# Sparse attention in pairs: the two heads of a feature block on two halves of TensorE's array

## The chip, the cores and the metric

The kernel runs on one core of a Trainium2 chip. The metric is the device time of one execution in microseconds (us). All data and all arithmetic of the part looked at here are float32.

## What is computed

The reference is two transformer stacks behind each other. The change touches one layer of the first stack, a sparse attention (NSA) over 512 tokens with 16 heads of 64 features, four heads sharing one group of keys and values. Each head attends three times: over 31 compressed blocks (`cmp`), over selected blocks (`slc`) and over a window (`win`). With 512 tokens there are 8 blocks of 64 and the top 16 are selected, so the selection takes all of them, and the window of 512 takes all earlier tokens: both are causal attention with a linear distance bias, each with keys and values of its own.

```
def nsa_attention(q, kc, vc, ks, vs, kw, vw, gate_logit, ...):
    ck = compress_kv(kc...)
    cv = compress_kv(vc...)
    ...
        sc = jnp.einsum('bqgrd,bcgd->bgrqc', qb, ck).astype(f32) * scale
        sc = jnp.where(ok_c, sc - slopes[:, :, None, None] * dist_c, NEG_INF)
        p_cmp = jnp.where(jnp.any(ok_c, axis=-1)[:, None], jax.nn.softmax(sc, axis=-1), 0.0)
        o_cmp = jnp.einsum('bgrqc,bcgd->bqgrd', p_cmp.astype(dt), cv)
        ...
        ss = jnp.einsum('bqgrd,bgqnld->bgrqnl', qb, kg).astype(f32) * scale
        ss = jnp.where(dist_s[:, :, None] >= 0, ss - slopes[...] * dist_s[:, :, None], NEG_INF)
        p_slc = jax.nn.softmax(ss.reshape(...), axis=-1).reshape(ss.shape)
        o_slc = jnp.einsum('bgrqnl,bgqnld->bqgrd', p_slc.astype(dt), vg)
        ...
        p_win = jax.nn.softmax(sw, axis=-1)
        o_win = jnp.einsum('bgrqk,bkgd->bqgrd', p_win.astype(dt), vwb)
        o = gb[..., 0:1] * o_cmp + gb[..., 1:2] * o_slc + gb[..., 2:3] * o_win
```

## The kernel before

Activations lie feature-major in SBUF: a feature block is 128 partitions by 512 tokens, and in this layer a block `pr` (0 to 7) of the queries holds two heads, `e` = 0 in partitions 0 to 63 and `e` = 1 in partitions 64 to 127 (`half(e)`). The list `NSA` (L338) writes out by hand the order of the work. Its entries are 128 jobs `("job", pr, i, e, br)`: query tile `i` (0 to 3, 128 queries) of head `e` against the `128*(i+1)` keys at or before it, for branch `br` (0 `slc`, 1 `win`); and 8 entries `("cmp", pr)`, the compressed branch of both heads and all query tiles of a block at once. Two query tiles alternate, 3 with 0 and then 2 with 1. The four jobs and the compressed part of one (pr, i) form a group `G`, which adds up its output in one PSUM bank.

Each job goes through six steps on three engines. TensorE: `scores` (L1311) writes queries times keys into one of three PSUM banks. VectorE: `highest` (L2716, the work at L2741) adds the distance bias, writes the result to `Sbuf` (four buffers) and keeps the row's extreme. ScalarE: `exps` (L2062) takes the exponential and the row sum. VectorE: `normalise` (L2744, reciprocal L2759, scaling by gate and sum L2761). TensorE: `turn` (L1327) transposes the rows in pieces of 128x128. ScalarE: `turned` (L2071, copy at L2082) brings them from PSUM to `PTbuf` (three buffers). TensorE: `values` (L1339) multiplies with the values at L1353 and adds into the group's bank; the first job of a group also adds the compressed part (L1350). When a group is complete, VectorE copies the bank out (`output`, L2763).

A scores matmul contracts over 64 partitions only, those of its head. A values matmul yields 64 features, but uses 128 columns of weights: `vpad_s` and `vpad_w` hold 192 columns for each key tile and group, the values in columns 64 to 127 and zeros on both sides, and a slice at 64 or at 0 puts the values into the lower or the upper half while zeros are added to the other half.

On TensorE the loop of slot n (L1361) issues scores(n+2), turn(n-2), values(n-3). Into 24 slots a quarter of a query projection is put, two matmuls 512 wide (`query_quarter`, L1299, `Q_PART`; slots 0 to 7 and every fifth up to 83). The waits that set the order: scores(n) waits for highest of job n-3, turn(n) for normalise(n) and for the copy of job n-2, values(n) for its own copy. highest(n) waits for scores(n) and for turn(n-4), whose buffer it takes. ScalarE issues exps(n) and then turned(n-2). VectorE issues highest(n), normalise(n-1), output(n-4), and near the end of the layer sums of weights and of inputs for the layer's output product `c_out` (n = 100, 101, 120, 124).

A float32 matmul is two instructions in the trace, each with a load of weights in front; a transpose is one.

Of the kernel before, what the change touches and what calls it, by code (L numbers as in the profile page):

```python
# [161 lines left out]
def build(nc, x_dram, mem_in, meta_in, w_tiles, w_narrow, w_cmp, consts, pick_halves, params, out, stop=None):  # L162
    ctx = ExitStack()
    with ctx:
# [148 lines left out]
        def half(h):  # L313
            return slice(64 * (h % 2), 64 * (h % 2) + 64)
# [24 lines left out]
        for _pr in range(8):  # L339
            for _a, _b in ((3, 0), (2, 1)):  # L340
                for _br, _e in ((0, 0), (0, 1), (1, 0), (1, 1)):
                    NSA += [("job", _pr, _i, _e, _br) for _i in (_a, _b)]
                if _a == 3 and _pr < 7:
                    NSA.append(("cmp", _pr + 1))
        NSA_JOB = [sum(t[0] == "job" for t in NSA[:n]) for n in range(len(NSA))]
        NSA_GROUPS = [(pr, i) for pr in range(8) for i in (3, 0, 2, 1)]
        CMP_AT = [NSA.index(("cmp", pr)) for pr in range(8)]
# [436 lines left out]
        def _(pe):  # L784
# [433 lines left out]
            def nsa():  # L1218
# [92 lines left out]
                def scores(n):  # L1311
                    if n >= 3:
                        pe.wait_ge(na_max, n - 2)
                    ps = sc_bank[n % 3]
                    if NSA[n][0] == "cmp":
                        pr = NSA[n][1]
                        arrived(pr)
                        for i in range(4):
                            mm = pe.matmul(ps[:, 64 * i:64 * i + 64], Z1[:, pr, P * i:P * i + P],
                                           ck[:, pr // 2].rearrange("p e n -> p (e n)"), start=True, stop=True)  # L1320
                    else:
                        _, pr, i, e, br = NSA[n]
                        mm = pe.matmul(ps[:, 0:P * (i + 1)], Z1[half(e), pr, P * i:P * i + P],  # L1323
                                       Z1[half(e), nsa_keys(pr, e, br), 0:P * (i + 1)], start=True, stop=True)
                    mm.then_inc(na_s, 1)
# [13 lines left out]
                def values(n):  # L1339
                    if NSA[n][0] == "cmp":  # L1340
                        return
                    _, pr, i, e, br = NSA[n]
                    g, G = pr // 2, nsa_group(pr, i)
                    o = PL[:, 2 * (G % 2), 0:P]
                    pe.wait_ge(na_pt, n + 1)
                    if (e, br) == (0, 0):
# [4 lines left out]
                    pad = slice(64, 192) if e == 0 else slice(0, 128)  # L1351
                    for j in range(i + 1):
                        mm = pe.matmul(o, (vpad_s, vpad_w)[br][:, j, g, pad], PTbuf[NSA_JOB[n] % N_BANK][:, P * j:P * j + P],  # L1353
                                       start=False, stop=(e, br) == (1, 1) and j == i)
                    mm.then_inc(na_v, 1)
# [3 lines left out]
                scores(0)  # L1359
                scores(1)  # L1360
                for n in range(len(NSA) + 3):  # L1361
                    if n + 2 < len(NSA):
                        scores(n + 2)
                    if n in Q_PART:
                        query_quarter(*Q_PART[n])
                    if 2 <= n < len(NSA) + 2:
                        turn(n - 2)
                    if n >= 3:
                        values(n - 3)
# [400 lines left out]
        def _(act):  # L1770
# [240 lines left out]
            def nsa(ready):  # L2011
# [59 lines left out]
                def turned(n):  # L2071
# [8 lines left out]
                    if m >= N_BANK:  # L2080
                        act.wait_ge(na_v, m - N_BANK + 1)
                    act.activation(PTbuf[m % N_BANK][:, 0:w], pt_bank[n % 2][:, 0:w], ACT.Copy).then_inc(na_pt, 1)  # L2082
# [282 lines left out]
        def _(dve):  # L2365
# [330 lines left out]
            def nsa():  # L2696
# [66 lines left out]
                def output(n):  # L2763
                    if NSA[n][0] == "cmp" or NSA[n][3:] != (1, 1):
                        return
# [4 lines left out]
                for n in range(len(NSA) + 4):  # L2770
# [6 lines left out]
                    if n >= 4:  # L2777
                        output(n - 4)
# [754 lines left out]
```

## Time and profile before

| | |
|---|---|
| median of 3 runs | 3782.35 us (3779.25 to 3784.62) |
| the profiled execution | 3778.26 us, its span 3776.4 us |
| busy share PE, DVE, ACT | 97%, 52%, 20% of the span |
| granted TensorE clock, mean | 0.978 (1.00 in the attention stage) |
| the attention stage | 1128 to 1420 us of the span, 292 us |
| in it: PE, DVE, ACT busy | 291.8, 174.0, 135.4 us |

A row of the timeline merges neighbouring instructions of a line: its start, the time to the end of the last, engine, line, operation, names, shapes (weights, then moving data) and count. Ends of matmuls are modelled (a matmul's record runs on over the start of the next), so what a block of matmuls costs TensorE is read from the start of one row to the start of the next row of PE. PEld is the load of weights.

### The profile page before, as it was taken

To read this page: it belongs to the slowest core of one execution; us is meant where nothing else is said; L and a number is where in the kernel's file an instruction comes from. 1 tells how busy PE (TensorE), PEld (TensorE's weight loads), DVE (VectorE), ACT (ScalarE), POOL (GpSimd) and SP (SyncE) were. 2 spreads that over 40 slices of the span, in tenths; PEclk is the share of its full clock that TensorE was granted. 3 is DMA by queue.
4 is the path that set the end of the run, shared out by engine and by line. 5 is a ranking of instruction groups with operands and counts; after the bars stand their busy time and mean duration, and the time that the engine had idled before them with its cause. 6 is when DMAs were issued, how large, how long until landed. Compare 5 with 4: busy or idle time off the path is not lost.

```text
span 3776.4 us, 43884 instructions
## 1 busy us (share of the span) xinstructions
PE 3658.8 (97%) x16715; PEld 2855.7 (76%) x16715; DVE 1978.3 (52%) x4623; ACT 757.3 (20%) x1849; POOL 70.5 (2%) x74
## 2 busy tenths in 40 slices
PE   8987999999999999999998999999999999999999
PEld 3374788888655668888886776888887888887766
DVE  4362366545205574675545547643344566557456
ACT  2221021100113451111001135022112111121143
POOL 0000000000000000000000011000000000000010
PEclk9998999999999999999998999999999999999999
DMA  3100312222210003212222110221110122101111
GB/s 125 56 12 25 120 56 79 89 89 90 100 45 12 12 12 112 78 68 90 86 82 78 67 45 23 81 76 67 45 45 34 67 78 85 39 23 68 56 45 45
DMA packets 35014, 236.83 MB, mean 63 GB/s; under 512 B 4716, under 2 KB 4844, under 8 KB 7168
## 3 DMA queue, kind: packets, MB, share of 16 engines
q1 hardware_dynamic: 31616, 224.41, 16.8%
q10 hardware_dynamic: 2704, 5.46, 0.4%
q0 software_dynamic: 496, 4.24, 0.3%
q8 instruction: 134, 2.20, 0.2%
q14 instruction: 64, 0.52, 0.0%
HBM read 232.00 MB, written 2.10 MB: 62 GB/s over the span
## 4 chain that ended last, share of the span: by engine, by line
PE 94%; DVE 4%; ACT 1%; issue 1%; DMA 0%; POOL 0%; ACTq 0%; POOLq 0%; DVEq 0%
PE PL L1193 25%; PE PX L1193 19%; PE PL L901 14%; PE PL L1572 4%; PE PL L1385 3%; PE PX L1323 2%; PE PL L885 2%; PE PL L1353 2%; PE PX L1675 2%; PE PL L1596 1%; PE PL L1306 1%; PE PL L1480 1%; PE PL L1718 1%; PE PX L1455 1%; PE PX L911 1%
## 5 line engine op out<-in xcount | busy, mean ns | idle before, releaser
L901 PE MATMUL PL<-xn,ring 128*128 128x264 f32 (+1 forms) x1600 | 508.8, 475 | 11.0 <-DVE xn L2394 9.8
L901 PEld LDWEIGHTS PL<-xn,ring 128*128 128x128 f32 x1600 | 306.5, 194 | 197.7 <-issue 164.8
L2437 DVE TENSOR_TENSOR Z<-PL,SCR 128x512 f32<-128x512 f32 (+3 forms) x104 | 63.9, 615 | 489.0 <-PE PL L901 377.6
L1193 PE MATMUL PL<-Z,ring 128*128 128x256 f32 (+1 forms) x1248 | 299.2, 391 | 2.1 <-POOL Z L3392 2.1
L1193 PEld LDWEIGHTS PL<-Z,ring 128*128 128x128 f32 x1248 | 242.8, 195 | 42.2 <-POOL Z L3392 2.4
L1193 PE MATMUL PL<-AUX,ring 128*128 128x256 f32 (+1 forms) x1056 | 243.9, 379 | 0.0
L1193 PEld LDWEIGHTS PL<-AUX,ring 128*128 128x128 f32 x1056 | 200.6, 190 | 27.6
L1193 PE MATMUL PL<-xn,ring 128*128 128x264 f32 (+1 forms) x864 | 204.3, 389 | 15.7 <-DVE xn L2394 14.5
L1193 PEld LDWEIGHTS PL<-xn,ring 128*128 128x128 f32 x864 | 165.8, 192 | 46.0 <-issue 12.4
L1849 ACT ACTIVATE SCR<-PL 128x256 f32<-128x256 f32 (+1 forms) x72 | 27.7, 384 | 739.1 <-PE PL L1193 739.1
L1193 PE MATMUL PX<-Z,AUX 128*128 128x264 f32 (+1 forms) x704 | 163.8, 384 | 0.5 <-DVE Z L3168 0.5
L1572 PE MATMUL PL<-xn,ring 128*128 128x264 f32 x640 | 154.1, 395 | 0.0
L1193 PE MATMUL PX<-AUX,ring 128*128 128x256 f32 (+1 forms) x640 | 152.5, 381 | 0.0
L1193 PEld LDWEIGHTS PX<-Z,AUX 128*128 128x128 f32 x704 | 133.7, 190 | 22.0 <-issue 0.8
L2584 DVE TENSOR_TENSOR SCR<-SCR,PL 128x256 f32<-128x256 f32 (+1 forms) x72 | 30.4, 422 | 214.3 <-PE PL L1193 214.3
L1572 PEld LDWEIGHTS PL<-xn,ring 128*128 128x128 f32 x640 | 121.5, 193 | 27.9 <-issue 7.9
L1193 PEld LDWEIGHTS PX<-AUX,ring 128*128 128x128 f32 x640 | 121.6, 190 | 17.8
L1819 ACT ACTIVATE SCR<-resid 128x512 f32<-128x512 f32 (+1 forms) x88 | 53.8, 632 | 384.2 <-DVEq L2626 239.7
L1385 PE MATMUL PL<-xn,ring 128*128 128x264 f32 x512 | 121.0, 393 | 0.0
L1385 PEld LDWEIGHTS PL<-xn,ring 128*128 128x128 f32 x512 | 98.7, 193 | 17.9 <-issue 0.7
L1323 PE MATMUL PX<-Z 64*128 64x512 f32 (+3 forms) x256 | 102.5, 481 | 0.0
L1849 ACT ACTIVATE AUX<-PL 128x264 f32<-128x264 f32 x44 | 17.2, 390 | 412.9 <-PE PL L1193 412.9
(517 smaller groups left out, 6386.1 us busy)
## 6 DMA issues: line engine op xcount, KB each, us to landing
ring<-w_tiles SPq DMA_DIRECT2D x212, 1024.0 KB, 4.8
cst<-consts ACTq DMA_DIRECT2D x1, 2252.5 KB, 15.0
resid<-x ACTq DMA_DIRECT2D x4, 512.0 KB, 8.3
AUX<-mem POOLq DMA_DIRECT2D x2, 1024.0 KB, 5.2
AUX<-w_cmp POOLq DMA_DIRECT2D x1, 2048.0 KB, 10.3
out<-resid SPq DMA_DIRECT2D x4, 512.0 KB, 5.1
par<-params ACTq DMA_DIRECT2D x1, 536.5 KB, 6.2
nar<-w_narrow ACTq DMA_DIRECT2D x1, 368.0 KB, 17.0
```

The source lines that it names most:

```text
L885: mm = pe.matmul(PL[:, 2 * h + c, 0:e - a], ring[t % 2][:, k, P * h:P * h + P], src[:, KB * kc + k, a:e], start=kc == 0 and k == 0, stop=k ...
L901: mm = pe.matmul(PL[:, 2 * h + c, 0:e - a], ring[t % 2][:, k, P * h:P * h + P], src_block(name, k)[:, a:e], start=k == 0, stop=k == KB - 1)
L911: mm = pe.matmul(PX[0:G, at + c, 0:e - a], K("sum_row", 7 - b // N["per"], 7 - b // N["per"] + G), sq_buf[:, bb % 4, a:e], start=b == 0, s ...
L1193: mm = pe.matmul(ps, lhs(k), rhs(k), start=kc == 0 and k == 0, stop=kc == per - 1 and k == 3)
L1323: mm = pe.matmul(ps[:, 0:P * (i + 1)], Z1[half(e), pr, P * i:P * i + P], Z1[half(e), nsa_keys(pr, e, br), 0:P * (i + 1)], start=True, stop ...
L1353: mm = pe.matmul(o, (vpad_s, vpad_w)[br][:, j, g, pad], PTbuf[NSA_JOB[n] % N_BANK][:, P * j:P * j + P], start=False, stop=(e, br) == (1, 1 ...
L1385: mm = pe.matmul(PL[:, 2 * h + c, 0:e - a], ring[t % 2][:, k, P * h:P * h + P], X2[:, k, a:e], start=k == 0, stop=k == KB - 1)
L1572: mm = pe.matmul(PL[:, 2 * c, 0:HALF], ring[t % 2][:, k, P * (u % 2):P * (u % 2) + P], X2[:, k, c * HALF:(c + 1) * HALF], start=k == 0, st ...
L1675: mm = pe.matmul(ps, k, q, start=True, stop=True)
L1819: act.activation(sq, src[b], ACT.Square).then_inc(norm_sq, 1)
L1849: act.activation(quad_work(name)[2 + n % 2], quad_bank(name, "m1"), ACT.Copy).then_inc(qd_c, 1)
L2437: ins = dve.tensor_tensor(d, ps, f, ALU.mult)
```

## The change

Jobs of the two heads of one (pr, i, br) become neighbours in `NSA` and form a unit; an entry `cmp` is a unit alone. TensorE's loop goes by units: scores of unit k+1 (both heads behind each other, in two banks), both turns of unit k-1, values of unit k-2. The values matmul takes the 64 columns that hold values and writes half of the partitions of the output; for each key tile the two heads' matmuls alternate, e = 0 into partitions 0 to 63, e = 1 into 64 to 127. The number of jobs, the turns, and all that VectorE and ScalarE do for a job stay as they are. There are four `PTpair` buffers in place of three `PTbuf`, and `output` is moved two slots back.

```
--- before.py
+++ after.py
@@ -338,12 +338,14 @@
         NSA = [("cmp", 0)]
         for _pr in range(8):
             for _a, _b in ((3, 0), (2, 1)):
-                for _br, _e in ((0, 0), (0, 1), (1, 0), (1, 1)):
-                    NSA += [("job", _pr, _i, _e, _br) for _i in (_a, _b)]
+                for _br in range(2):
+                    NSA += [("job", _pr, _i, _e, _br) for _i in (_a, _b) for _e in range(2)]
                 if _a == 3 and _pr < 7:
                     NSA.append(("cmp", _pr + 1))
         NSA_JOB = [sum(t[0] == "job" for t in NSA[:n]) for n in range(len(NSA))]
         NSA_GROUPS = [(pr, i) for pr in range(8) for i in (3, 0, 2, 1)]
+        NSA_UNITS = [(n,) if t[0] == "cmp" else (n, n + 1) for n, t in enumerate(NSA) if t[0] == "cmp" or t[3] == 0]
+        PTpair = [SCR[:, 512 * (N_S + j):512 * (N_S + j + 1)] for j in range(4)]
         CMP_AT = [NSA.index(("cmp", pr)) for pr in range(8)]
         C_FIRST = 14
         Q_SLOTS = list(range(8)) + [8 + 5 * j for j in range(16)]
@@ -1308,21 +1310,23 @@
                     if part == 3:
                         mm.then_inc(lin_done, 1)
 
-                def scores(n):
-                    if n >= 3:
-                        pe.wait_ge(na_max, n - 2)
+                def scores(unit):
+                    n = unit[0]
                     ps = sc_bank[n % 3]
+                    if unit[-1] >= 3:
+                        pe.wait_ge(na_max, unit[-1] - 2)
                     if NSA[n][0] == "cmp":
                         pr = NSA[n][1]
                         arrived(pr)
                         for i in range(4):
                             mm = pe.matmul(ps[:, 64 * i:64 * i + 64], Z1[:, pr, P * i:P * i + P],
                                            ck[:, pr // 2].rearrange("p e n -> p (e n)"), start=True, stop=True)
-                    else:
+                        mm.then_inc(na_s, 1)
+                        return
+                    for n in unit:
                         _, pr, i, e, br = NSA[n]
-                        mm = pe.matmul(ps[:, 0:P * (i + 1)], Z1[half(e), pr, P * i:P * i + P],
-                                       Z1[half(e), nsa_keys(pr, e, br), 0:P * (i + 1)], start=True, stop=True)
-                    mm.then_inc(na_s, 1)
+                        pe.matmul(sc_bank[n % 3][:, 0:P * (i + 1)], Z1[half(e), pr, P * i:P * i + P],
+                                  Z1[half(e), nsa_keys(pr, e, br), 0:P * (i + 1)], start=True, stop=True).then_inc(na_s, 1)
 
                 def turn(n):
                     pe.wait_ge(na_nrm, n + 1)
@@ -1336,37 +1340,38 @@
                             mm = pe.transpose(pt_bank[n % 2][:, P * j:P * j + P], Sbuf[n % N_S][:, P * j:P * j + P], ident)
                     mm.then_inc(na_tps, 1)
 
-                def values(n):
-                    if NSA[n][0] == "cmp":
+                def values(unit):
+                    if NSA[unit[0]][0] == "cmp":
                         return
-                    _, pr, i, e, br = NSA[n]
+                    _, pr, i, e, br = NSA[unit[0]]
                     g, G = pr // 2, nsa_group(pr, i)
                     o = PL[:, 2 * (G % 2), 0:P]
-                    pe.wait_ge(na_pt, n + 1)
-                    if (e, br) == (0, 0):
+                    pe.wait_ge(na_pt, unit[1] + 1)
+                    if br == 0:
                         if G >= 2:
                             pe.wait_ge(na_done, G - 1)
                         pe.wait_ge(na_pt, CMP_AT[pr] + 1)
                         pe.matmul(o, cv[0:64, g, :], cPT[pr % 2][:, P * i:P * i + P], start=True, stop=False)
-                    pad = slice(64, 192) if e == 0 else slice(0, 128)
                     for j in range(i + 1):
-                        mm = pe.matmul(o, (vpad_s, vpad_w)[br][:, j, g, pad], PTbuf[NSA_JOB[n] % N_BANK][:, P * j:P * j + P],
-                                       start=False, stop=(e, br) == (1, 1) and j == i)
-                    mm.then_inc(na_v, 1)
+                        for e, n in enumerate(unit):
+                            mm = pe.matmul(o[half(e)], (vpad_s, vpad_w)[br][:, j, g, 64:128],
+                                           PTpair[NSA_JOB[n] % 4][:, P * j:P * j + P], start=False, stop=br == 1 and j == i)
+                    mm.then_inc(na_v, 2)
 
                 pe.wait_ge(t_sb, nt[0])
                 pe.wait_ge(psum_free, u0 + 2 + C_FIRST)
-                scores(0)
-                scores(1)
-                for n in range(len(NSA) + 3):
-                    if n + 2 < len(NSA):
-                        scores(n + 2)
-                    if n in Q_PART:
-                        query_quarter(*Q_PART[n])
-                    if 2 <= n < len(NSA) + 2:
-                        turn(n - 2)
-                    if n >= 3:
-                        values(n - 3)
+                scores(NSA_UNITS[0])
+                for k in range(len(NSA_UNITS) + 2):
+                    if k + 1 < len(NSA_UNITS):
+                        scores(NSA_UNITS[k + 1])
+                    for n in (NSA_UNITS[k] if k < len(NSA_UNITS) else ()):
+                        if n in Q_PART:
+                            query_quarter(*Q_PART[n])
+                    if 1 <= k <= len(NSA_UNITS):
+                        for n in NSA_UNITS[k - 1]:
+                            turn(n)
+                    if k >= 2:
+                        values(NSA_UNITS[k - 2])
                 quadrants("c_out", [(na_done, 31)], source=(na_done, 0, 4))
 
             def window(i):
@@ -2077,9 +2082,9 @@
                         act.activation(cPT[pr % 2], pt_bank[n % 2][0:64, :], ACT.Copy).then_inc(na_pt, 1)
                         return
                     m, w = NSA_JOB[n], P * (NSA[n][2] + 1)
-                    if m >= N_BANK:
-                        act.wait_ge(na_v, m - N_BANK + 1)
-                    act.activation(PTbuf[m % N_BANK][:, 0:w], pt_bank[n % 2][:, 0:w], ACT.Copy).then_inc(na_pt, 1)
+                    if m >= 4:
+                        act.wait_ge(na_v, m - 3)
+                    act.activation(PTpair[m % 4][:, 0:w], pt_bank[n % 2][:, 0:w], ACT.Copy).then_inc(na_pt, 1)
 
                 for n in range(len(NSA) + 2):
                     if n < len(NSA):
@@ -2761,21 +2766,21 @@
                     dve.tensor_scalar(S, S, rc[n % N_S], gates[:, i, at:at + 1], ALU.mult, ALU.mult).then_inc(na_nrm, 1)
 
                 def output(n):
-                    if NSA[n][0] == "cmp" or NSA[n][3:] != (1, 1):
+                    if n >= len(NSA) or NSA[n][0] == "cmp" or NSA[n][3:] != (1, 1):
                         return
                     _, pr, i, e, br = NSA[n]
                     dve.wait_ge(na_v, NSA_JOB[n] + 1)
                     dve.tensor_copy(A1[:, 4 + pr, P * i:P * i + P], PL[:, 2 * (nsa_group(pr, i) % 2), 0:P]).then_inc(na_done, 1)
 
-                for n in range(len(NSA) + 4):
+                for n in range(len(NSA) + 6):
                     if n < len(NSA):
                         highest(n)
                     if 1 <= n <= len(NSA):
                         normalise(n - 1)
                     if n in Q_PART and Q_PART[n][1] == 3:
                         projected(Q_PART[n][0], 3)
-                    if n >= 4:
-                        output(n - 4)
+                    if n >= 6:
+                        output(n - 6)
                     if n in (100, 101):
                         weight_sums("c_out", 0, n - 100)
                     if n == 120:
```

## Rows read from the trace of the kernel before

**Rows 1.** The page, part 4: the chain that ended last, by engine.
```profile
PE 94%; DVE 4%; ACT 1%; issue 1%; DMA 0%; POOL 0%; ACTq 0%; POOLq 0%; DVEq 0%
```
**Rows 2.** Windows, busy us (instructions): whole stage; one block with query quarters, one without.
```profile
core 0: us, PE busy (x) PEld busy (x) DVE busy (x) ACT busy (x) POOL busy (x), PEclk, DMA share, GB/s
...
1128.00:1420.00 292.00, 291.75 (x1473) 186.23 (x1473) 174.00 (x637) 135.42 (x402) 0.00 (x0) 1.00 0.04 14
...
1225.09:1261.53 36.44, 36.44 (x187) 23.32 (x186) 21.17 (x79) 16.69 (x51) 0.00 (x0) 1.00 0.08 30
...
1364.92:1396.05 31.13, 31.13 (x173) 21.02 (x173) 22.28 (x81) 16.70 (x51) 0.00 (x0) 1.00 0.00 1
```
**Rows 3.** Waits of the stage, 1128 to 1420: total us, times, longest.
```profile
ACT SCR L2082 <- PE PX L1336: 66.8, 54, 3.4
...
DVE tiny L2759 <- ACT SCR L2069: 23.8, 62, 0.7
...
PEld PX L1336 <- DVE SCR L2761: 8.1, 14, 0.8
```
**Rows 4.** Timeline of PE alone, 1224 to 1231.
```profile
1224.03 0.49 PE L1350 MATMUL PL<-AUX 64*128 64x128 f32 x2
1224.44 1.16 PE L1353 MATMUL PL<-SCR,Z 128*128 128x128 f32 x8
1225.53 1.12 PE L1323 MATMUL PX<-Z 64*128 64x512 f32 x2
1226.58 0.66 PE L1336 MATMUL PL<-cst,SCR 128*128 128x128 f32 x4
1227.17 0.48 PE L1350 MATMUL PL<-AUX 64*128 64x128 f32 x2
...
1228.59 1.06 PE L1353 MATMUL PL<-SCR,Z 128*128 128x128 f32 x8
1229.48 1.00 PE L1319 MATMUL PX<-AUX,Z 128*128 128x64 f32 x8
1230.32 0.61 PE L1336 MATMUL PL<-cst,SCR 128*128 128x128 f32 x4
1230.76 0.39 PE L1353 MATMUL PL<-SCR,Z 128*128 128x128 f32 x2
```
**Rows 5.** Timeline of PE, start of the stage: two scores behind each other.
```profile
1129.26 1.34 PE L1323 MATMUL PX<-Z 64*128 64x512 f32 x4
1130.54 1.55 PE L1306 MATMUL PL<-xn,ring 128*128 128x512 f32 x3
```
**Rows 6.** Timeline of PE before the stage: weights of 64 columns.
```profile
1093.90 0.60 PE L1248 MATMUL PX<-cst,Z 128*128 128x128 f32 x4
1094.43 0.68 PE L1272 MATMUL PX<-par,AUX 128*64 128x64 f32 x8
1095.04 0.70 PE L901 MATMUL PL<-xn,ring 128*128 128x512 f32 x1
```
**Rows 7.** Groups of the stage by shape: busy us, mean ns, idle before.
```profile
L1353 PE MATMUL PL<-SCR,Z 128*128 128x128 f32 x640 | 95.6, 280 | 0.0
...
L1323 PE MATMUL PX<-Z 64*128 64x512 f32 x64 | 35.9, 641 | 0.0
```
**Rows 8.** Timeline of all engines, 1364 to 1370: the way of one job.
```profile
1366.99 0.66 PE L1336 MATMUL PL<-cst,SCR 128*128 128x128 f32 x4
...
1367.68 0.60 ACT L2082 ACTIVATE SCR<-PL 128x512 f32<-128x512 f32 x1 [2.08 <-PE PL L1336]
1367.80 0.69 DVE L2741 CUSTOM_DVE_ANT_0 SCR<-AUX,PX 128x512 f32<-128x512 f32 x1 [1.41 <-PE PL L1336]
...
1368.18 0.39 ACT L2069 ACTIVATE SCR<-SCR,tiny 128x128 f32<-128x128 f32 x1
...
1368.69 0.16 DVE L2759 RECIPROCAL tiny<-tiny 128x1 f32<-128x1 f32 x1 [0.20 <-ACT SCR L2069]
...
1368.89 0.34 DVE L2761 TENSOR_SCALAR SCR<-SCR,tiny,AUX 128x128 f32<-128x128 f32 x1
```

## The prediction

> **What bounds the kernel now.** I read the page's chain first: TensorE carries 94% of it [rows 1]. The windows then show the stage that the change touches: in 292.0 us TensorE is busy for 291.75, VectorE for 174.0, ScalarE for 135.4 [rows 2]. Busy ends of matmuls are modelled, so I looked at who waits for whom: ScalarE's copies wait 67 us for turns in one of the two banks, while TensorE's wait for a normalised row adds up to only 8.1 us in 14 times [rows 3]. The others wait for TensorE. What TensorE saves here comes off the time, until another engine is late. The stage is eight blocks (two heads each, 16 jobs and one compressed entry): 31.13 us for one without query quarters, 36.44 with three [rows 2].
>
> **TensorE's price list.** Read from start to start of the blocks of one line. Eight values instructions take 0.89 us where their neighbours have the same shape (1228.59 to 1229.48), so 0.111 each; eight others take 1.09 between blocks of 64 rows (1224.44 to 1225.53): 0.20 more [rows 4]. Four turns take 0.44 between equal neighbours (1230.32 to 1230.76) and 0.59 (1226.58 to 1227.17) between 64-row blocks: 0.11 each, and 0.15 more [rows 4]. A scores pair 512 wide takes 1.05 between others [rows 4]: less 0.20 that is 0.427 per instruction, 0.107 per key tile of 128. Two scores of one head behind each other, 512 and 128 wide, take 1.28 (1129.26 to 1130.54) [rows 5], where 2 x 0.427 + 2 x 0.107 = 1.07: the 0.2 falls due once. So a switch of shape costs 0.20 into a matmul and 0.15 into a turn, and staying costs nothing. Eight instructions with 64 columns of weights and 64 moving take 0.61 (1094.43 to 1095.04), less some 0.14 for the switch: 0.058 each [rows 6], so a load of 64 columns costs half of one of 128.
>
> **Check on one block of today.** Scores: 4 jobs of each width, 2 instructions each: 2 x 0.107 x (1+2+3+4) x 4 = 8.56. Turns: 40 x 0.111 = 4.44. Values: 80 x 0.111 = 8.9. Switches: 16 jobs x (0.20 + 0.15) = 5.6. Compressed part of values, four times 0.21 and two switches of 0.20 (0.41 from 1224.03 to 1224.44 is one and the work [rows 4]): 2.44. Compressed entry, scores 0.84 (1229.48 to 1230.32) and four turns 0.44 [rows 4]: 1.28. Sum 31.2, measured 31.13 [rows 2]. The list holds.
>
> **The change, part by part.** Pairing (both scores, both turns, both values): a pair has one way into scores, one into turns and one into values, 0.20 + 0.15 + about 0.145 (into 64-column weights), 0.495 for each of 8 units = 3.96, in place of 5.6. The compressed part costs 4 x (0.20 + 0.21) = 1.66, since its second switch is now the one into the values. Turns and compressed entry stay, 4.44 and 1.28.
> Values: the number of instructions stays (640 [rows 7]); their weights are 64 columns. Nothing in the trace of before shows two halves of the array at work, so the price is bounded from both sides. If they do not overlap, the 128 moving columns set 0.109 each, 8.75 for a block. If they do, the loads of 0.058 set it: 80 x 0.058 = 4.64.
> Scores: again no row. Without overlap 8.56. With it, instructions start in the order written: first and second of head 0, first and second of head 1. The second of head 0 needs the place of its first, the first of head 1 can run beside it, and the second of head 1 comes after: three lengths in place of four, 6.42, and 0.2 for one-tile units, where four loads of 0.107 are longer: 6.6.
> Block without overlap: 8.56 + 4.44 + 8.75 + 3.96 + 1.66 + 1.28 = 28.65, 2.5 less than 31.13. With overlap: 6.6 + 4.44 + 4.64 + 3.96 + 1.66 + 1.28 = 22.6, 8.5 less. I take overlap: neither half reads or writes what the other does in the array; heads' scores lie in different banks and values in different partitions. The query quarters stay, with the same neighbours.
> The page "TensorE: Matmul & The Clock Gate" of the Trainium skill, Part 3, says that matmuls of different tiles run concurrently but start and end strictly in order; no run here shows it yet. It agrees with three lengths for scores, and its measured 2.38x for three column tiles would put values nearer 5.5 than 4.64.
>
> **What becomes late.** VectorE's 22.28 us for a block [rows 2] do not change and are now as long as TensorE's 22.6. Two chains return to TensorE. (a) Scores of the next unit wait for the highest of this unit's first job, which waits for the turn two units back. A highest starts 0.15 us after a turn's end, takes 0.69 [rows 8] and needs about 0.1 to be seen; the end itself lies 0.27 after the last turn's start: 1.2. TensorE has meanwhile the second turn 0.44 and the values of a one-tile unit, about 0.4: it waits 0.3 in each second unit, unless a compressed part (0.41) fills it. (b) A turn waits for its normalised row: copy of the unit before (1367.68 to 1368.18), exponential until the reciprocal at 1368.69, scaling to 1369.23 [rows 8]: 1.9 from the last turn's start, TensorE's own work between is 1.7, and (a) is inside it. Together about 0.6 per block. The compressed entry gives VectorE more work than TensorE in its place. I take 1.3 us of waits per block; bounds are 0 and 3. The upper one is VectorE's 22.3 plus its own waits for ScalarE, 23.8 / 8 = 3.0 [rows 3], 25.3 against 22.6. The moved `output` waits for the values of a unit already issued, behind it stand two steps of VectorE; the fourth buffer and the reordered list cost no instruction. A pipeline of units fills and drains about 2 us longer, and VectorE's sums for `c_out` in the last blocks, hidden today, cost 1. The following product starts when the last output is copied, as now, so the gain passes on.
>
> **Sum.** 8 x (8.5 - 1.3) = 58, less 3: 55 us. The profiled execution of 3778.26 would be 3723; the median of the runs is 4 higher: 3782 - 55 = 3727. Its own range goes from 8 x 8.5 = 68 to 8 x 5.5 - 3 = 41 us saved: 3714 to 3741; if both heads' scores even began together, VectorE would be the bound and little more be won.
>
> **The rivals.**
> No overlap, only fewer switches: 8 x 2.5 less 1 = 19 us, 3763. For it: float32 is two instructions, and no row shows halves together. Against: nothing shared that I can name. 0.15.
> One of the two overlaps. Scores alone: 19 + 8 x 1.96 = 35, 3747; values alone: 19 + 8 x 4.1 less waits = 46, 3736. Two heads' scores read different partitions, two heads' values the same 128, so scores are the safer part. 0.10.
> Slower: a change of half costs as a change of shape does. Rows 5 show free neighbours only on one half. A block has 32 changes in values (1, 3, 5, 7 per unit, two branches) and 8 in scores. At 0.145 and 0.20 that is 4.6 + 1.6 = 6.2, less the 2.5 saved: 3.7 x 8 = 30 us more, 3812; at 0.20 throughout 44 more, 3826. It turns into a loss from 2.5 / 40 = 0.06 us per change. 0.07.
> The page "TensorEngine Tiling (Array Packing)" of the Trainium skill, Key Properties, says that a change of mode drains TensorE and a change of tile does not: the 0.20 agree with the first half, and by the second this rival falls.
> Slower by loads: if a load for one column half cannot go beneath the other's matmul, values cost 0.109 + 0.055 each, 13.1 per block: 33.0 against 31.13, 15 us more, 3797. Rows 6 speak against: 64-column loads there lie beneath matmuls. 0.02.
> The same page on TensorE, Part 3, says that loads overlap running matmuls only where the row group differs, which two column halves do not do; by the trace, full-width loads overlap in the same rows (0.111 per instruction).
> No gain: the chains (a) and (b) grow so long that they eat the 2.5 per block: 3780. They are 1.2 and 1.9 beside units of 3.6. 0.03.
>
> **How the numbers follow.** Overlap in both 0.63, in one 0.10, none 0.15, these are faster: 0.88. Within 0.2% (7.6 us, about what a measurement of this kernel tells from no change) 0.03. Slower 0.09. The range 3710 to 3766 holds the three faster cases but for their edges, about 0.8.
>
> **What would show it.** After the change the values of a four-tile pair (16 instructions) take about 1.0 us to the next block's start with overlap, 1.9 without, over 3 if changing halves costs. Scores of a wide pair: 1.6 with three lengths, 2.05 without overlap. A block without quarters takes 23 to 25 us, or 28.7. VectorE's busy share in it goes from 72% to over 90%, ScalarE's long waits for turns shrink, TensorE's waits for normalised rows grow to 1 or 2 us per block. The granted clock stays 1.00. I am wrong if instructions of two halves are a full length apart, or if a block's length is set by VectorE above 25.

## The result

| | before | after |
|---|---|---|
| median of the runs | 3783.05 us (4 runs, 3779.25 to 3784.62) | 3713.66 us (4 runs, 3708.36 to 3716.06) |
| span of the profiled execution | 3776.4 us | 3706.5 us |
| the stage, first scores of a job to first matmul of `c_out` | 290.7 us (1129.26 to 1419.96) | 222.5 us (1127.69 to 1350.15) |
| behind the stage | 2356.5 us | 2356.4 us |

The ratio is 0.9821 with a 95% interval of 0.9803 to 0.9839: 69 us less, where 55 was forecast. The stage gives 68.2 of them; the stretch behind it has not moved. Against the medians of the kernel before in the later comparisons (3779 to 3780, of 7 to 13 runs) it is 66 us.

The windows of the changed kernel, columns as in [rows 2]: the whole stage, a block with three query quarters, a block with none.

```profile
core 0: us, PE busy (x) PEld busy (x) DVE busy (x) ACT busy (x) POOL busy (x), PEclk, DMA share, GB/s
1127.69:1350.15 222.46, 209.39 (x1465) 125.19 (x1464) 167.23 (x637) 128.59 (x401) 0.00 (x0) 0.98 0.05 16
1205.65:1232.94 27.29, 25.91 (x186) 15.62 (x185) 20.35 (x82) 15.88 (x50) 0.00 (x0) 1.00 0.12 40
1286.91:1311.63 24.72, 22.22 (x174) 14.04 (x173) 21.91 (x85) 15.99 (x50) 0.00 (x0) 0.93 0.01 1
```

The same work of VectorE, 21.9 us in a block against 22.3, now fills 24.7 us, 89% in place of 72%, and TensorE is no longer busy throughout: 22.2 of 24.7. The waits of the changed kernel, 1121 to 1346 (engine, what it wants to start, who released it; total us, times, longest):

```profile
ACT SCR L2087 <- PE PL L1340: 40.1, 22, 6.1
ACT SCR L2087 <- PE PX L1340: 30.9, 26, 2.8
...
PEld PX L1328 <- DVE tiny L2746: 18.7, 34, 2.2
...
PEld PX L1340 <- DVE SCR L2766: 11.0, 19, 0.8
```

The same waits before, 1128 to 1420, of which [rows 3] has only the first and the third:

```profile
ACT SCR L2082 <- PE PX L1336: 66.8, 54, 3.4
ACT SCR L2082 <- PE PL L1336: 66.3, 51, 3.9
...
PEld PX L1336 <- DVE SCR L2761: 8.1, 14, 0.8
...
PEld PL L1336 <- DVE SCR L2761: 4.9, 10, 0.8
...
PEld PX L1323 <- DVE tiny L2741: 1.7, 3, 0.8
```

Over both groups of banks (PX and PL) the copies wait 71 us for turns in place of 133. A new wait stands high up: the loads of the scores (L1328) wait 18.7 us for a highest (L2746), 1.7 before. The timeline of PE shows what the blocks of TensorE cost now, from the start of one row to the start of the next:

```profile
1227.07 0.88 PE L1357 MATMUL PL<-SCR,Z 128*64 128x128 f32 x12
1227.88 1.13 PE L1328 MATMUL PX<-Z 64*128 64x512 f32 x4
1228.94 0.66 PE L1340 MATMUL PX<-cst,SCR 128*128 128x128 f32 x4
...
1231.92 1.09 PE L1357 MATMUL PL<-SCR,Z 128*64 128x128 f32 x16
1232.94 1.10 PE L1322 MATMUL PX<-AUX,Z 128*128 128x64 f32 x8
```

Scores of a pair of heads, four instructions 512 wide, take 1.06 us (1227.88 to 1228.94). One head, two instructions, took 1.05 [rows 4]: the second head costs nothing. Values of a four-tile pair, 16 instructions, take 1.02 us (1231.92 to 1232.94); eight took 0.89 to 1.09 [rows 4]. In the trace the four instructions of that scores pair start at 1227.878, .884, 1228.411 and .418. The last two carry the increments of the semaphore, so they are the second instructions of both heads: the first of head 1 starts 0.007 us after the first of head 0, the second of head 0 one length after its own first, and that of head 1 0.007 us later again.

### The profile page after: what moved, and what is told of

It reads as the page before. It is cut to its first block, busy times and chain, and to the rows that moved or that the text cites. A ratio compares the mean times of both kernels' runs of the same rounds, so it can differ in the third digit from the quotient of the medians.

```text
span 3706.5 us, 43883 instructions
## 1 busy us (share of the span) xinstructions
PE 3574.4 (96%) x16715; PEld 2793.0 (75%) x16715; DVE 1970.5 (53%) x4623; ACT 751.3 (20%) x1849; POOL 70.5 (2%) x74
## 4 chain that ended last, share of the span: by engine, by line
PE 92%; DVE 5%; ACT 2%; issue 1%; DMA 0%; POOL 0%; ACTq 0%; POOLq 0%; DVEq 0%
PE PL L1195 26%; PE PX L1195 19%; PE PL L903 14%; PE PL L1577 4%; PE PL L1390 3%; PE PL L887 2%; PE PX L1680 2%; PE PL L1601 1%; PE PL L1308 1%; PE PL L1485 1%; PE PX L1328 1%; PE PL L1723 1%; PE PX L1460 1%; PE PX L913 1%; PE PL L1357 1%
## 5 line engine op out<-in xcount | busy, mean ns | idle before, releaser
L903 PE MATMUL PL<-xn,ring 128*128 128x264 f32 (+1 forms) x1600 | 505.3, 473 | 12.0 <-DVE xn L2399 10.8
L1195 PEld LDWEIGHTS PX<-Z,AUX 128*128 128x128 f32 x704 | 133.7, 190 | 21.9 <-issue 0.8
L1195 PE MATMUL PL<-Z,AUX 128*128 128x264 f32 (+1 forms) x352 | 88.4, 396 | 6.7 <-DVE AUX L2503 3.4
```

The source lines that it names most:

```text
L903: mm = pe.matmul(PL[:, 2 * h + c, 0:e - a], ring[t % 2][:, k, P * h:P * h + P], src_block(name, k)[:, a:e], start=k == 0, stop=k == KB - 1)
L1195: mm = pe.matmul(ps, lhs(k), rhs(k), start=kc == 0 and k == 0, stop=kc == per - 1 and k == 3)
```

## The experiments

Execution times differ by some 4 to 6 us either way from run to run, while the length of the stage in the trace repeats block by block: four blocks, from one compressed entry to the next (1148.13 to 1262.40), take 31.16, 26.36, 27.29 and 29.46 us in the changed kernel, and within 0.02 us the same in three of the kernels below, which differ from it only further on. So both are given: the median, and the stage against 222.5 us. Where the granted clock of the stage is below 1.00, stretches at 1.2 GHz are in it. The changed kernel has two of 3.4 us each, from 1300.7 and from 1331.4. Such a stretch can cost up to half its length, and as each kernel has one trace, it is not known whether they would fall the same way again: a difference of 2 or 3 us in the stage says little where they differ.

**Values not on halves.**

```
-                            mm = pe.matmul(o[half(e)], (vpad_s, vpad_w)[br][:, j, g, 64:128],
+                            mm = pe.matmul(o, (vpad_s, vpad_w)[br][:, j, g, (slice(64, 192), slice(0, 128))[e]],
...
```

> The changed kernel with one part undone: values use 128 columns of weights again (zeros for the other head's half), still alternating between the heads, and so cannot run on two halves. Pairs, scores and order stay. Theory A (overlap of values is worth 80 x (0.111 - 0.055) = 4.5 us of TensorE per block, and TensorE sets the time in the blocks with query quarters, another loop in the last three): 5 blocks x 4.5 less 1 of waits that vanish, and in the last three, where the blocks take 24.5 to 25.4 us against 20 of TensorE work, only some 0.5 to 1: stage 223.5 + 20 = about 243, time 3712 + 20 = 3732, 16 instructions of values take 1.8 to 2.0 us. Rival B (TensorE alone sets all blocks): 8 x 4.5 = 36 us more, 3748.

Measured: 3733.1 us, ratio to before 0.9885 (0.9868 to 0.9903). Stage and timeline of PE:

```profile
1129.59:1376.53 246.94, 237.79 (x1466) 165.92 (x1466) 167.91 (x637) 128.93 (x401) 0.00 (x0) 0.99 0.04 14
```
```profile
1243.89 2.05 PE L1357 MATMUL PL<-SCR,Z 128*128 128x128 f32 x16
1245.78 0.45 PE L1322 MATMUL PX<-AUX,Z 128*128 128x64 f32 x3
```

16 instructions take 1.89 us in place of 1.02, the stage is 24.4 us longer, the time 19 us. So overlapping values are worth 19 to 24 us, near the 20 of theory A and not 36. But the 36 of rival B overlooks that full-width values have the shape of the turns. In the 32 units without a compressed part this kernel drops the switch of 0.145 us between them, and in the 32 others its switch is 0.20 in place of 0.145: 8 x 4.5 - 4.6 + 1.8 = 33 us, and added up from the blocks of both traces 32. Of these the stage shows 24, so TensorE's work sets most of it. The late part is not spared, as A had it: the block with the last two quarters (24.5 us in the changed kernel) is 3.7 us longer, and the two and a half behind it together 4.9 (24.7 and 38.5 us became 25.9 and 42.2), although they have 6.8 us at 1.2 GHz in the changed kernel and none here.

**Scores not on halves.** One wait more, in `scores`:

```
                     for n in unit:
                         _, pr, i, e, br = NSA[n]
+                        if e:
+                            pe.wait_ge(na_s, n)
```

> The changed kernel with one wait added: the scores of head 1 wait until those of head 0 are complete, so they cannot overlap. Theory A (two lengths in place of four are what overlap gives to scores, 0.214 x (i+1) per pair): 4.3 us per block and about 0.25 us for each of 8 waits, 2 us: in five blocks with quarters + 6, in the last three + 2 to 3 since they are not set by TensorE: 3712 + 37 = 3749. Rival B (overlap in the records is only in how they are noted, and scores took the same engine time before): + 8 x 2 = 16 us, 3728.

Measured: 3770.1 us, ratio 0.9975 (0.9965 to 0.9984).

```profile
1134.72:1415.69 280.97, 267.93 (x1466) 148.14 (x1465) 169.63 (x637) 128.51 (x401) 0.00 (x0) 0.95 0.04 13
```
```profile
1231.46 1.88 PE L1330 MATMUL PX<-Z 64*128 64x384 f32 x4
1233.27 1.98 PE L1308 MATMUL PL<-xn,ring 128*128 128x512 f32 x4
```

A pair 384 wide takes 1.81 us; in the changed kernel 0.84 (1237.41 to 1238.25). The 0.97 are two lengths of 0.32 and 0.33 for the wait. Over 64 units that is 34 + 21 = 55 us, 6.9 per block. The stage is 58.5 us longer, more than theory A's 37, but not by these 55 alone. Two of its blocks, with the granted clock last but two:

```profile
1302.60:1333.68 31.08, 30.19 (x182) 17.09 (x180) 20.65 (x80) 15.89 (x51) 0.00 (x0) 1.00 0.10 35
1333.68:1368.41 34.73, 32.74 (x174) 18.85 (x173) 22.49 (x83) 16.12 (x52) 0.00 (x0) 0.80 0.00 1
```

The first, wholly at 2.4 GHz, is 6.6 us longer than in the changed kernel (24.51), and the three other such blocks 5.9 to 6.5: about 50 us for the stage. The second, the next one, is 10.0 us longer (24.72), with 13.7 us at 1.2 GHz. In all, 27 us of this stage ran at 1.2 GHz, 7 in the changed kernel: these 20 us more can cost up to 10, and are the likely rest. Theory A was low because the wait costs 0.33 and not 0.25, because later blocks did not hide it, and by the clock. The records do show engine time; B falls. Nearly the whole gain goes in this kernel, but of the 58.5 us about 21 are the price of the added wait and about 8 probably the clock, which leaves some 30 for the overlap of scores.

**The old order with 64 columns of weights.** The values line of the kernel before alone:

```
-                    pad = slice(64, 192) if e == 0 else slice(0, 128)
...
-                        mm = pe.matmul(o, (vpad_s, vpad_w)[br][:, j, g, pad], PTbuf[NSA_JOB[n] % N_BANK][:, P * j:P * j + P],
+                        mm = pe.matmul(o[half(e)], (vpad_s, vpad_w)[br][:, j, g, 64:128], PTbuf[NSA_JOB[n] % N_BANK][:, P * j:P * j + P],
```

> The kernel before with one part of the change alone: values use the 64 columns that hold values and write half of the partitions, in the old order, one head per slot, so that no two halves stand next to each other. Theory A (only the moving columns set the price of 0.109 to 0.111 per instruction, and the switch into 64-column weights is 0.145 in place of 0.20): 128 x 0.055 = 7 us and 640 x 0.002 = 1 us less: 3775. Rival B (64-column weights alone make each instruction cheaper, 0.058): 640 x 0.05 = 32 us less, 3750.

Measured: 3793.8 us, ratio 1.0047 (1.0028 to 1.0065): slower, and both theories said faster. The stage is 302.8 us, 12.1 longer than before. First a turn of the kernel before (the row behind it starts at 1228.59, [rows 4]), then the same place here:

```profile
1228.42 0.33 PE L1336 MATMUL PX<-cst,SCR 128*128 128x128 f32 x1
```
```profile
1231.94 0.33 PE L1336 MATMUL PX<-cst,SCR 128*128 128x128 f32 x1
1232.20 1.09 PE L1352 MATMUL PL<-SCR,Z 128*64 128x128 f32 x8
1233.21 0.99 PE L1319 MATMUL PX<-AUX,Z 128*128 128x64 f32 x7
```

The turn's one instruction now takes 0.26 to the next row, where 0.17 stood before, and eight values 1.01 in place of 0.89. Turns and full-width values had the same shape; in the 96 jobs without a compressed part there was no switch between them, and now there is one, which both of my expectations overlooked. 96 x 0.145 = 13.9, less 1.8 for the cheaper switch of the 32 others and 1.3 for 640 instructions of 0.109: 10.8 against 12.1 measured; the compressed entries, now behind values of another shape, are not in that sum. Half-width weights alone are a loss; they pay only beside their other half.

**How near must the halves stand?** Two other orders of the values, first all tiles of head 0 and then of head 1, then in stretches of two tiles:

```
-                    for j in range(i + 1):
-                        for e, n in enumerate(unit):
+                    for e, n in enumerate(unit):
+                        for j in range(i + 1):
```
```
+                    for j, e, n in [(j, e, n) for jj in range(0, i + 1, 2) for e, n in enumerate(unit) for j in range(jj, min(jj + 2, i + 1))]:
```

> The changed kernel, values with 64 columns but not alternating: all key tiles of head 0, then all of head 1. The trace of the changed kernel shows both instructions of a float32 matmul of head 0 interleaved with those of head 1, 7 ns apart, and scores of a wide pair done in two lengths where I had forecast three. Theory A (TensorE starts strictly in program order of whole matmuls and only neighbours overlap): of 4 tiles per head one overlaps, 16 instructions take about 1.65 us in place of 1.02, stage + 15 us or so, time 3727. Rival B (TensorE looks ahead and takes from both halves whatever is queued): no change, values still 1.02 us for 16, 3712.

> The changed kernel, values with 64 columns in another order: two key tiles of head 0, two of head 1, and so on. With the heads alternating by tile, 16 instructions take 1.02 us; with all of one head first they take 1.51, and there the first instruction of head 1 starts beside the fifth of eight of head 0, while three of head 0 have yet to start. Theory A (TensorE starts what is queued for the other half as long as no more than three earlier instructions are pending): four instructions per stretch are within that reach, 16 take 1.05 to 1.1 us, stage within 2 us of 222.5. Rival B (overlap only at the seam between two stretches, by a fixed amount of about five lengths in 16): 1.25 us or more, stage + 4 us.

Measured: 3715.5 us (ratio 0.9837, 0.9820 to 0.9854) and 3707.5 us (0.9816, 0.9799 to 0.9833). First head by head, then by two tiles, PE:

```profile
1231.20 1.58 PE L1357 MATMUL PL<-SCR,Z 128*64 128x128 f32 x16
1232.71 1.10 PE L1322 MATMUL PX<-AUX,Z 128*128 128x64 f32 x8
```
```profile
1231.25 1.15 PE L1356 MATMUL PL<-SCR,Z 128*64 128x128 f32 x16
1232.33 1.10 PE L1322 MATMUL PX<-AUX,Z 128*128 128x64 f32 x8
```

16 instructions take 1.51 us head by head, between A's 1.65 and B's 1.02. Neither theory had it. The starts tell the rule: eight run from 1231.20 to 1232.01, the later ones 0.109 apart, which must be head 0's, and head 1's first starts at 1231.69, beside the fifth, while three of head 0 that stand ahead of it in the program have yet to start. With six instructions per head it starts beside the third (1226.36), with four beside the first (1229.26): three pending each time. So TensorE starts an instruction for the free half past others that wait for the busy half, and its reach here was three of them. In stretches of two tiles (four instructions) that reach is enough: 1.08 us, and a stage of 223.2 against 222.5. Head by head the stage is 229.9, 7 us longer; the medians alone don't tell these kernels from the changed one.

This is also why scores take two lengths. The Trainium skill ("TensorE: Matmul & The Clock Gate", Part 3) has matmuls start strictly in program order, which would put head 1's first behind head 0's second, three lengths; here the start of head 1's first lies 0.53 us ahead of it (1227.884 and 1228.411), and the measurement decides.

**What sets the last blocks.** Additional work of VectorE, late and early: the reciprocal is taken three times.

```
-                    step(dve.reciprocal(rc[n % N_S], sm[n % N_S]))
+                    for _ in range(3 if n >= 84 else 1):
+                        step(dve.reciprocal(rc[n % N_S], sm[n % N_S]))
```

(for the early one `32 <= n < 84`)

> The changed kernel; in the 50 jobs from slot 84 on, behind the last query quarter, VectorE takes the reciprocal three times in place of once: 2 x 0.2 us per job, 20 us more of its work, result the same. Theory A (from there on VectorE and the chains through it set the time, 22 us of VectorE work in blocks of 24.7): 14 to 20 us more, about 3730. Rival B (TensorE sets it there too, as before the change): its 20 us of work in a block of 24.7 leave 4.7 idle, 3 blocks hide 14 of the 20, 5 us more.

> The counterpart of e5_dve_late: the same two additional reciprocals of 0.2 us, now in the 49 jobs of slots 32 to 83, where query quarters are still put in; 19.6 us more of VectorE's work, result the same. In e5_dve_late 20 us of such work lengthened the stage by 14.7 us. Theory A (in these blocks TensorE has 20.0 us of attention and 5.2 or more of quarters in 26.4 to 29.5 us, VectorE 20; the addition brings VectorE to 27 us per block and is mostly covered): stage + 2 to 7 us, 3718. Rival B (the chains through VectorE set the pace here too): + 12 to 20 us, 3728.

Measured: late 3725.6 us (0.9861, 0.9846 to 0.9876), stage 237.2; early 3719.9 us (0.9837, 0.9814 to 0.9860), stage 230.4.

```profile
1129.86:1367.07 237.21, 213.91 (x1465) 126.75 (x1465) 181.40 (x737) 130.60 (x401) 0.00 (x0) 0.97 0.04 15
```
```profile
1135.11:1365.55 230.44, 210.96 (x1465) 125.45 (x1464) 181.40 (x735) 130.53 (x401) 0.00 (x0) 0.99 0.05 15
```

Of 20 us of work the stage shows 14.7 if it comes late and 8.0 of 19.6 if it comes early. By the medians it is 12 and 6 us. Late it is mostly VectorE's pace that counts, as theory A said; the early figure lies just above A's 2 to 7, so even beside the quarters the two engines are close. The late one has some 6 us more at 1.2 GHz than the changed kernel, the early one no more than it, so up to 3 of the 14.7 may be the clock. Nor does VectorE set the last blocks alone: the values at full width showed that TensorE's work lengthens them too.

**Can the waits be arranged away?** Five kernels: quarters every 4.25 slots; sums for `c_out` one by one; both; the sums and a fourth bank for scores from slot 88; the sums and the turns ahead of the scores. Of the edits the lines that move the work are shown; the functions that issue single sums, the choice of the bank and the order of the last kernel are left out.

```
-        Q_SLOTS = list(range(8)) + [8 + 5 * j for j in range(16)]
+        Q_SLOTS = [5 + int(4.25 * j) for j in range(24)]
```
```
-                    if n in (100, 101):
-                        weight_sums("c_out", 0, n - 100)
-                    if n == 120:
-                        dve.wait_ge(na_done, 24)
-                        sums_head("c_out", 0, (0, 3))
-                    if n == 124:
-                        sums_tail("c_out", 0, (0, 3))
+                    if n in (94, 96, 98, 100):
+                        one_weight_sum(n // 2 - 47)
+                    if n in (113, 115, 117, 119):
+                        one_input_sum((n - 113) // 2)
```
```
-                        pe.wait_ge(na_max, unit[-1] - 2)
+                        pe.wait_ge(na_max, max(SC_PREV[m] for m in unit) + 1)
+                    if 3 in [SC_AT[m] for m in unit]:
+                        arrived(7)
```

> The changed kernel with one list altered: the 24 query quarters, today in slots 0 to 7 and every fifth up to 83, lie every 4.25 slots from 5 to 102, so that TensorE's extra work reaches into the stretch where it waits. Theory A (first part bound by TensorE, last three blocks by VectorE with TensorE idle 4 us in each): 6 to 8 of the quarters' 10 us move into idle time: 5 us less, 3708. Rival B (waits come from the two chains and appear wherever TensorE's work is short): no gain, within 2 us of 3713.

> The changed kernel; VectorE's sums for the layer's output product, today three of 0.68 us in a row at slot 100 and pairs of 0.95 at 120 and 124, are issued one by one with two slots between. Theory A (each bundle holds back the next highest, scores wait up to 2 us for it, as the trace of the changed kernel shows at 1298 to 1300, and the granted clock falls to 1.2 GHz right after): two waits of 2 us become about four of 0.3, and the two slow stretches go, 2 x 1.5 us: 4 to 6 us less, 3708. Rival B (VectorE's total sets the stretch, however it is arranged): no change.

> Both of the arrangements in one kernel, quarters spread and sums one by one. Theory A (they are two different losses, both in the last three blocks): the gains add in part, 7 to 9 us less than the changed kernel, about 3705, stage 222.5 to 214. Rival B (the loss is VectorE's sum of work): no more than 2 us.

> The changed kernel with the sums one by one (the arrangement of e7_sums_spread) and, from slot 88 on, when the bank of the query product is free, four PSUM banks for scores in place of three, so that the scores of a unit wait for the unit before the last and not for the first job of the last. Theory A (of 20 us in which the loads of the scores wait for a highest, the 10 in the last three blocks come from the third bank): stage 220.5 less 3 to 6 = 214.5 to 217.5, time 3706 to 3709. Rival B (VectorE is as busy as it can be there, waits only move to the turns): stage within 1 us of 220.5.

> The changed kernel with the sums one by one and with TensorE's order in a step altered from scores(k+1), turns(k-1), values(k-2) to turns(k-1), scores(k+1), values(k-2); work and switches are the same in number. Theory A (the scores' waits for the highest, 20 us in the stage, are those of the chain turn, highest, scores, to which the turns are now added as cover): 3 to 8 us less than 220.5. Rival B (the turns then wait longer for their normalised rows, which come through two more steps of VectorE): within 2 us or slower, up to 226.

| | median us | ratio, 95% interval | stage us |
|---|---|---|---|
| quarters spread | 3711.7 | 0.9828 (0.9812 to 0.9844) | 228.0 |
| sums one by one | 3711.9 | 0.9823 (0.9808 to 0.9837) | 220.5 |
| both | 3710.6 | 0.9820 (0.9807 to 0.9833) | 222.7 |
| sums, fourth bank | 3707.9 | 0.9816 (0.9802 to 0.9829) | 221.2 |
| sums, turns first | 3719.3 | 0.9845 (0.9832 to 0.9859) | 229.7 |

The timeline of the changed kernel shows what the sums do. VectorE's three sums (L2497 to L2500) stand ahead of a highest, TensorE waits for that, and its next matmuls are slow:

```profile
1297.69 0.88 PE L1357 MATMUL PL<-SCR,Z 128*64 128x128 f32 x12
...
1298.03 0.68 DVE L2497 TENSOR_TENSOR Z<-ring 128x512 f32<-128x512 f32 x1
...
1298.63 0.68 DVE L2498 TENSOR_TENSOR ring<-ring 128x512 f32<-128x512 f32 x1
1299.23 0.68 DVE L2500 TENSOR_TENSOR Z<-Z,ring 128x512 f32<-128x512 f32 x1
1299.83 0.41 DVE L2746 CUSTOM_DVE_ANT_0 SCR<-AUX,PX 128x256 f32<-128x256 f32 x1
...
1300.30 0.30 PEld L1328 LDWEIGHTS PX<-Z 64*128 64x128 f32 x4 [1.98 <-DVE tiny L2746]
1300.31 1.75 PE L1328 MATMUL PX<-Z 64*128 64x512 f32 x4 [1.74 <-DVE tiny L2746]
...
1301.98 0.90 PE L1340 MATMUL PL<-cst,SCR 128*128 128x128 f32 x3
```

The wide pair takes 1.67 us to the next row in place of 1.06, and the window of this block has a granted clock of 0.93: a stretch at 1.2 GHz after TensorE had stood still for 2 us. With the sums one by one the stage has no such stretch, and is 2 us shorter; I had expected 4 to 6. The freed time is not TensorE's to use. In 60 of that kernel's last 61 us VectorE is 90% busy, and TensorE by its modelled ends 89%:

```profile
1295.00:1355.00 60.00, 53.39 (x446) 34.21 (x447) 53.88 (x205) 42.04 (x131) 0.00 (x0) 1.00 0.01 2
```

With the fourth bank part of the waits moves. The same 60 us of work in both kernels, 1295 to 1355 with three banks and 1291 to 1351 with four (where L1347 is the turn, L2773 the scaling, L1335 the scores and L2753 highest):

```profile
PEld PX L1328 <- DVE tiny L2746: 9.7, 15, 1.6
...
PEld PX L1340 <- DVE SCR L2766: 4.4, 8, 0.8
PEld PL L1340 <- DVE SCR L2766: 3.2, 6, 0.8
```
```profile
PEld PX L1347 <- DVE SCR L2773: 6.9, 10, 1.5
PEld PL L1347 <- DVE SCR L2773: 4.6, 7, 1.6
...
PEld PX L1335 <- DVE tiny L2753: 0.8, 4, 0.2
```

Of the 9.7 us of the scores 1 is left (0.2 of it in the bank of the other group), and 11.5 us stand at the turns, where 7.6 were: together about 5 us less. The stage is no shorter all the same, 221.2 against 220.5, but 6.8 us of it (from 1324.0) ran at 1.2 GHz, which can cost 3.4, and nothing of the other did. So the number is B's, waits do move along the chain, and whether the bank is worth some 3 us at 2.4 GHz throughout stays open.

Spreading the quarters gave nothing. By itself the stage is 5.5 us longer (five blocks of 28.6 to 28.9 us, then one of 31.6), with 13.7 us at 1.2 GHz; with the sums one by one it is 222.7 against 220.5 for the sums alone. Turns first make the stage 9 us longer than the sums alone: VectorE now waits 39 us for scores. I know of no arrangement that is faster than the changed kernel beyond the uncertainty; the sums with the fourth bank and the values by two tiles have the lowest medians, 3708, with intervals that overlap the changed kernel's.

## Why the prediction was right, and where its terms were off

- TensorE sets the stage: right. Its work went down, and the time with it. The price list from [rows 4 to 6] held: switches 0.20 and 0.15, loads of 64 columns beneath the other half's matmuls. The switch into 64-column weights, 0.145, stood in no row of before; 16, 12, 8 and 4 such instructions now take 1.02, 0.81, 0.59 and 0.37 us, which is 0.054 each and 0.15 for the switch.
- Values: 80 x 0.058 = 4.64 per block was forecast; (1.02 - 0.145) / 16 = 0.055 gives 4.4. Right.
- Scores: the step that failed. I let the program's order forbid head 1's first instruction to start before head 0's second, three lengths, 6.6 per block. Runs showed two: 8.56 / 2 = 4.28. That is 2.3 x 8 = 18.6 us more gain. The range named this case ("if both heads' scores even began together"), but said that VectorE would leave little of it; it left most (18.6 less the 6.6 of additional waits, below).
- A block's work is thus 4.28 + 4.44 + 4.4 + 3.96 + 1.66 + 1.28 = 20.0 us and not 22.6. With 24 quarters of 1.77 ((36.44 - 31.13) / 3, [rows 2]) TensorE's sum is 202.5 of 222.5 us.
- Waits: the other 20 us, of which up to 3.4 are the 6.8 us at 1.2 GHz and the rest waits; 13.4 was forecast (8 x 1.3 and 3). I had read TensorE's waits for a normalised row from one group of banks, 8.1 us; with the other they were 13.0 before, and 15.3 after, so these hardly grew. What is new are the scores' 18.7. The kind was right, highest before scores and normalised row before turns. With TensorE at 20 us per block, VectorE's 22 were the longer, which the term had not allowed for; the last one and a half blocks alone take 38.5 us for 30 of work, and I gave fill, drain and sums only 3.
- Sum: 55 + 18.6 + 1.9 (values) - 6.6 = 68.9 us, measured 68.2. So 3727 was 13 us too slow, and two misses of opposite sign are in it. The measured 3713.7 lies at the very edge of the 3714 to 3741 of my own case. Without the 6.6 us of further waits it would have been about 3707, outside 3710 to 3766 too: that the range held is in part luck.
- The rivals: no overlap and one overlap fell by the trace and by the runs without it. That a change of half costs a switch fell: 16 alternating instructions take 1.02 us, not over 3. That loads for one column half cannot go beneath the other's matmuls fell with the same 1.02. The worth of each part, by undoing it in the changed kernel: values on halves 24 us of stage, scores on halves some 30 (50 in blocks at 2.4 GHz, less 21 for the added wait). As far as such parts add up, that leaves some 14 us for pairs and their fewer switches (19 was forecast for them alone). Pairs alone were not run, nor was the fourth buffer or the moved `output` by itself.
- I foresaw 23 to 25 us for a block without quarters: 24.7. The granted clock in it was not the 1.00 that I foresaw, but 0.93.

## What to carry to other kernels

Price a stage of TensorE from start to start of its blocks, with a price for each change of shape: that list forecast all parts that had a row, and forgetting one change of shape (turn to half-width values) turned an expected gain into a loss of 15 us. Two halves of the array double the rate of float32 matmuls with 64 rows or 64 columns if the two streams stand close to each other in the program, within three instructions here. Before counting on the whole, hold the new sum of TensorE against the next engine's: here 20 against 22 us per block, and of five attempts to arrange the last 20 us away none gained beyond the uncertainty.

## What the runs showed of the hardware that I had not expected

- Matmuls for two row halves, or two column halves, start 0.007 us apart and run at full rate each. TensorE lets one for the free half start past three that wait for the busy half; at four instructions a stretch the overlap is nearly whole (1.08 us for 16 against 1.02), at eight it is less than half (1.51, where 1.89 is none).
- Waiting on a semaphore between two scores of a pair costs 0.33 us beyond the lost overlap.
- After TensorE had stood still for 2 us in the late blocks the granted clock went to 1.2 GHz and a wide scores pair took 1.67 us in place of 1.06. In the kernel with the sums one by one, where the longest wait of the scores' loads was 1.9 us (1.6 in the late blocks), the stage stayed at 2.4 GHz. No rule follows from this: TensorE stood still for 1.66 us at 1245 in the changed kernel without a change of the clock, and the same 1.66 us, at 1258.5 in the kernel with full-width values, were followed by 3.4 us at 1.2 GHz.
